# Six norms of a two-block transformer kernel, taken in two halves of the tokens

## The chip, the core and the metric

The kernel runs on one core of one Trainium2 chip. The metric is the time of one execution on the device in microseconds, and the median of the runs is what is compared. The engines are TensorE (PE, products), VectorE (DVE), ScalarE (ACT), GpSimd (POOL) and SyncE (SP, which issues the loads). They run side by side and wait for one another by semaphores only.

## What is computed

512 tokens of width 1024 pass through a block with a convolution mixer and a pooling mixer, and then through a block with a Fourier mixer, a feed-forward layer, a retention mixer with four heads, a second feed-forward layer and a final norm. The context branch of the reference doesn't reach the output and isn't computed. Cut to what matters here:

```python
def _rms(x, g):
    return x * lax.rsqrt(jnp.mean(x * x, axis=-1, keepdims=True) + EPS) * g

# between two mixers, six times (n1 to n6; n0 is the one at the start):
x = x + gate[:, None, :] * (y @ w_out)                 # leaves the last product of a stage
h = rmsnorm(x, norm_g) * (1.0 + scale[:, None, :]) + shift[:, None, :]
... = h @ w_in                                          # first product of the next stage

# gate, scale and shift come from a product of the condition vector:
mod = silu(c) @ w_ada[i] + b_ada[i]
```

## The kernel before

Everything lies transposed: x is [128, 8, 512], eight chunks of 128 features by 512 tokens. Every operand of a product is kept as two float32r parts, hi and lo, and a product is three matmuls, hi by hi, hi by lo, lo by hi (`three`, L1278 to L1280). An output tile is 128 features by 512 tokens in one PSUM bank, eight chunks of features deep, that is 24 matmuls of 512 columns. Four banks are in use at a time, so tiles come in fours (`four_tiles`). The last part of a feed-forward layer is six chunks deep, the last retention projection four, with two tiles in a unit.

Weights come in units of 128 x 1024, four slots. SyncE loads a unit into w_raw, ScalarE rounds it to w_hi (`refill`, L516), GpSimd subtracts to get w_lo (L425). `refill(name, s)` fills the slot that tile s of `name` has left, and stands in ScalarE's own order where the code writes it. The modulation vectors are summed by VectorE from groups of four 512 KB blocks (`sum_mods`, L892), each group loaded into the ring that the group before it leaves; these calls stand between VectorE's evictions.

A stage ends in `out`: TensorE makes eight tiles (the first four with their chunks interleaved, as the input comes), VectorE adds each to x (L921), ScalarE squares it (L525), VectorE adds the square to ssum (L856). Then `stat` brings the sums to one number per token (L1335), ScalarE takes the root, VectorE the reciprocal and four diagonals (L864), `spread` brings them back over the partitions into ps_bc (L1353), and `norm` makes for each chunk m_buf (L877, one input in PSUM), h_hi on ScalarE (L541) and h_lo (L881, both tensor inputs in SBUF). The next stage's first four tiles follow the chunks as they come (`h_part`). `keep_busy` issues products whose result nobody reads (L1329), one at a statistic and two behind a spread.

What follows a norm is the pooling stage (n1; VectorE's window sums, which ScalarE's refills wait for), the Fourier stage (n2; its products go through `ab_hi`, `ab_lo`, L1105), feed-forward (n3, n5), retention (n4; `rotary`, L1172 on) and the output (n6; L820 and eight stores). The order on each engine is the order in which the code is written; nothing reorders it.

## Time and profile before

| | us |
|---|---|
| median of 3 runs | 1791.09 |
| lowest, highest | 1789.49, 1798.33 |
| profiled execution | 1794.07 |
| its span | 1792.3 |
| PE busy in the span | 1682.2 |
| DVE busy | 896.0 |
| ACT busy | 588.0 |
| POOL busy | 753.9 |

A busy share is an average over stages that have different limits. What one stage could gain is read from the stretches in which the fullest engine waits, and from what ends those waits. The granted clock of TensorE over the span was 0.962 of full speed. A line number is that of the kernel before; the line of a helper serves many places.

### The profile page before, as it was taken

Reading aid. Unit: us, or ns where it says so; the run is one execution under the profiler, and the core shown is the slowest. Engines: PE = TensorE matmul, PEld = TensorE weight load, DVE = VectorE, ACT = ScalarE, POOL = GpSimd, SP = SyncE. Lnnn points to the kernel's source line nnn. Section 1 sums busy time; section 2 is a strip of 40 time slices with the busy share of each in tenths; the row PEclk is TensorE's granted clock in tenths of the full one; section 3 lists DMA queues with packets and bytes.
Section 4 is the critical chain, followed back from the end, with each engine's and each line's share of the span. In section 5 each row is a group of like instructions: output and inputs, shape, how many; then the busy total and the mean of one; then the engine's idle time right before and its main releaser. Section 6 shows DMA issues by size and latency. Waiting matters only on the chain.

```text
span 1792.3 us, 21415 instructions
## 1 busy us (share of the span) xinstructions
PE 1682.2 (94%) x7244; PEld 1355.9 (76%) x7244; DVE 896.0 (50%) x1369; ACT 588.0 (33%) x772; POOL 753.9 (42%) x354
## 2 busy tenths in 40 slices
PE   6999598899798999999998999999999899999997
PEld 4786386777666888888886878888787688888886
DVE  7999888876457534333357245171543511111114
ACT  4434442243222432222233333342333342222233
POOL 4799431454024344444444323334232253544442
PEclk8999698999898999999998999999999899999999
DMA  7431254376046455555552222222121132322321
GB/s 296 167 141 59 94 205 165 126 248 225 24 141 235 166 197 188 188 187 202 177 195 94 81 71 78 85 82 92 60 93 48 47 106 82 117 94 85 112 77 56
DMA packets 65149, 232.31 MB, mean 130 GB/s; under 512 B 7232, under 2 KB 7232, under 8 KB 64960
## 3 DMA queue, kind: packets, MB, share of 16 engines
q1 hardware_dynamic: 65088, 231.50, 37.6%
q8 instruction: 38, 0.62, 0.1%
q14 instruction: 23, 0.19, 0.0%
HBM read 229.38 MB, written 2.10 MB: 129 GB/s over the span
## 4 chain that ended last, share of the span: by engine, by line
issue 61%; POOL 26%; PE 2%; POOLq 1%; ACT 0%; DVE 0%; DVEq 0%
POOL w_lo L425 25%; POOL cv_y L498 1%; PE bank L1278 1%; PE bank L1279 1%; PE bank L1280 1%; POOLq L424 0%; POOLq L501 0%; ACT x L820 0%; POOL cv_y L491 0%; DVE m_buf L877 0%; PE ps_bc L1353 0%; PE ps_stat L1335 0%; PE ps_bc L1329 0%; DVE x L921 0%; ACT sq L525 0%
## 5 line engine op out<-in xcount | busy, mean ns | idle before, releaser
L425 POOL TENSOR_TENSOR w_lo<-w_raw,w_hi 128x1024 fp32r<-128x1024 f32 x272 | 662.2, 2440 | 995.0 <-ACT w_hi L516 974.7
L1278 PE MATMUL bank<-h_hi,w_hi 128*128 128x512 f32 x1344 | 531.4, 395 | 18.6 <-POOL w_lo L425 11.7
L1279 PE MATMUL bank<-h_lo,w_hi 128*128 128x512 f32 x1344 | 526.3, 392 | 0.0
L1280 PE MATMUL bank<-h_hi,w_lo 128*128 128x512 f32 x1344 | 526.2, 392 | 0.0
L516 ACT ACTIVATE w_hi<-w_raw 128x1024 fp32r<-128x1024 f32 x268 | 281.4, 1052 | 272.1 <-PE bank L1280 252.1
L1278 PEld LDWEIGHTS bank<-h_hi,w_hi 128*128 128x128 f32 x1344 | 254.4, 189 | 81.5 <-POOL w_lo L425 15.7
L1280 PEld LDWEIGHTS bank<-h_hi,w_lo 128*128 128x128 f32 x1344 | 254.2, 189 | 53.9
L1279 PEld LDWEIGHTS bank<-h_lo,w_hi 128*128 128x128 f32 x1344 | 254.4, 189 | 53.5 <-issue 1.1
L1278 PE MATMUL bank<-f_hi,w_hi 128*128 128x512 f32 x624 | 246.4, 395 | 8.7 <-POOL w_lo L425 4.0
L1279 PE MATMUL bank<-f_lo,w_hi 128*128 128x512 f32 x624 | 245.3, 393 | 0.0
L1280 PE MATMUL bank<-f_hi,w_lo 128*128 128x512 f32 x624 | 244.8, 392 | 0.0
L1144 DVE TENSOR_TENSOR z_buf<-bank,s_buf 128x512 f32<-128x512 f32 x44 | 30.4, 692 | 314.0 <-PE bank L1280 314.0
L892 DVE CUSTOM_DVE_ANT_0 mods_ring<-mods_ring,c_all 128x1024 f32<-128x1024 f32 x144 | 167.7, 1214 | 7.3 <-DMA mods_ring<-w_mods_in 7.0
L546 ACT ACTIVATE f_hi<-z_buf 128x512 fp32r<-128x512 f32 (+1 forms) x100 | 62.7, 630 | 283.8 <-DVE z_buf L1144 190.9
L921 DVE SCALAR_TENSOR_TENSOR x<-bank,mod,x 128x512 f32<-128x512 f32 x80 | 59.8, 747 | 174.3 <-PE bank L1280 174.3
L1278 PEld LDWEIGHTS bank<-f_hi,w_hi 128*128 128x128 f32 x624 | 118.4, 190 | 36.4 <-POOL w_lo L425 5.7
L1280 PEld LDWEIGHTS bank<-f_hi,w_lo 128*128 128x128 f32 x624 | 118.7, 190 | 25.1
L1279 PEld LDWEIGHTS bank<-f_lo,w_hi 128*128 128x128 f32 x624 | 118.7, 190 | 24.5
L913 DVE TENSOR_TENSOR f_lo<-z_buf,f_hi 128x512 fp32r<-128x512 f32 (+1 forms) x100 | 80.9, 810 | 52.1 <-ACT f_hi L546 50.8
L525 ACT ACTIVATE sq<-x 128x512 f32<-128x512 f32 x48 | 30.3, 632 | 153.5 <-DVE x L921 153.5
L1005 DVE SCALAR_TENSOR_TENSOR ps_bc<-cv_y,vec,ps_bc 128x512 f32<-128x512 f32 (+1 forms) x111 | 74.8, 674 | 0.0
L1005 DVE SCALAR_TENSOR_TENSOR ps_stat<-cv_y,vec,ps_stat 128x512 f32<-128x512 f32 (+1 forms) x111 | 74.8, 674 | 0.0
(177 smaller groups left out, 1520.1 us busy)
## 6 DMA issues: line engine op xcount, KB each, us to landing
mods_ring<-w_mods_in SPq DMA_DIRECT2D x152, 512.0 KB, 5.9
w_raw<-ff_in_in SPq DMA_DIRECT2D x88, 512.0 KB, 3.3
w_raw<-ret_in SPq DMA_DIRECT2D x64, 512.0 KB, 3.3
w_raw<-ff_out_in SPq DMA_DIRECT2D x32, 512.0 KB, 3.3
w_raw<-cv_ab_in SPq DMA_DIRECT2D x16, 512.0 KB, 5.2
w_raw<-ff_tail_in SPq DMA_DIRECT2D x16, 384.0 KB, 3.1
w_raw<-cv_g_in SPq DMA_DIRECT2D x8, 512.0 KB, 3.3
w_raw<-cv_out_in SPq DMA_DIRECT2D x8, 512.0 KB, 5.3
```

The source lines that it names most:

```text
L425: pool.tensor_tensor(w_lo[:, s, :], w_raw[:, s, :], w_hi[:, s, :].bitcast(F32), ALU.subtract).then_inc(lo_done, 1)
L516: act.activation(w_hi[:, u % SLOTS, :], w_raw[:, u % SLOTS, :], ACT.Copy).then_inc(hi_done, 1)
L525: act.activation(sq[:], src, ACT.Square).then_inc(sq_ready, 1)
L546: act.activation(dst, z_buf[:, q, :], ACT.Copy).then_inc(zh_ready, 1)
L892: v.tensor_tensor_reduce(out=mods_ring[:, s, :], in0=mods_ring[:, s, :], in1=c_all[:], scale=1.0, scalar=0.0, op0=ALU.mult, op1=ALU.add, a ...
L913: v.tensor_tensor(dst, z_buf[:, q, :], hi, ALU.subtract).then_inc(zl_ready, 1)
L921: v.scalar_tensor_tensor(x[:, j, :], bank[j % SLOTS][:], gate(n, j), x[:, j, :], ALU.mult, ALU.add).then_inc(left[j % SLOTS], 1)
L1005: v.scalar_tensor_tensor(acc(q, n), cv_y[:, bass.ds(k + (c * ROW + a), n)], vec[:, bass.ds(DC * k + (V_DW + c), 1)], acc(q, n), ALU.mult, ...
L1144: v.tensor_tensor(z_buf[:, q, :], bank[2 * q + 1][:], s_buf[:, q, :], ALU.mult).then_inc(left[2 * q + 1], 1)
L1278: pe.matmul(out, w_h, m_h, start=start, stop=False)
L1279: pe.matmul(out, w_h, m_l, start=False, stop=False)
L1280: return pe.matmul(out, w_l, m_h, start=False, stop=stop)
```

## The change

The tokens are handled in two halves of 256 at n1 to n6. The last four tiles of a stage's last product are made for tokens 0 to 255 first (two tile halves in one bank) and then for tokens 256 to 511. Behind the first half, VectorE and ScalarE evict, square and normalise the first half of the tokens, while TensorE makes the second half, with the statistic and the spread of the first half between its tile halves. The next stage's first four tiles are made for the first half of the tokens, in pairs of banks, with the statistic and the spread of the second half between them, and then for the second. The filler products at the six norms go. The modulation sums that stood ahead of every second or fourth tile stand ahead of the first two or four tiles, group 9 is loaded earlier, and the Fourier stage makes its tiles in another order (`ab_place`). The six are n1 to n6, by the map OUT_OF. The core of the diff:

```diff
+HALF = [slice(0, HT), slice(HT, T)]
+OUT_OF = {"cv_out": 1, "pl_out": 2, "fr_out": 3, "out02": 4, f"ro{HEADS - 1}": 5, "out12": 6}
@@ sync
             mods(8)
+            mods(9)
             four(later("pl_v", 0), t["pl_v"], 0)
...
-            mods(9)
...
-            for c in range(DC):
-                sp.wait_ge(out_ready, c + 1)
-                sp.dma_start(t["y_t"][:, c, :], x[:, c, :]).then_inc(y_out, 16)
+            for hf in range(2):
+                for c in range(0, DC, 2):
+                    sp.wait_ge(out_ready, DC * hf + c + 2)
+                    sp.dma_start(t["y_t"][:, c:c + 2, HALF[hf]], x[:, c:c + 2, HALF[hf]]).then_inc(y_out, 16)
@@ scalar
+            def out_and_norm(name, per_unit=1):
+                n = OUT_OF[name]
+                load_table(ACT.Sqrt)
+                for j in range(SLOTS):
+                    wait_left(act, name, j)
+                    square(f"n{n}", j, x[:, j, :])
+                    if j % per_unit == per_unit - 1:
+                        refill(name, j // per_unit)
+                half_squares(name, 0)
+                half_std(n, 0)
+                if per_unit == 1:
+                    refill(name, 4)
+                norm_part(n, 0, 0, 3)
+                refill(name, 5 if per_unit == 1 else 2)
+                norm_part(n, 0, 3, 6)
+                if per_unit == 1:
+                    refill(name, 6)
+                norm_part(n, 0, 6, 8)
+                refill(name, 7 if per_unit == 1 else 3)
+                half_squares(name, 1)
+                half_std(n, 1)
+                norm_part(n, 1, 0, DC)
@@ vector
+            def half_norm(n, hf):
...
+                for c in range(DC + 1):
+                    if c < DC:
...
+                        v.scalar_tensor_tensor(m_buf[:, c % 2, h], x[:, c, h], aff[:, c:c + 1], ps_bc[:, h],
                                                ALU.mult, ALU.mult).then_inc(m_ready, 1)
+                    if c and n < 6:
+                        v.wait_ge(hh_ready, H0[n] + DC * hf + c)
+                        v.scalar_tensor_tensor(h_lo[:, c - 1, h], m_buf[:, (c - 1) % 2, h],
                                                mod[:, SHIFT[n] + c - 1:SHIFT[n] + c],
+                                               h_hi[:, c - 1, h].bitcast(F32), ALU.add,
                                                ALU.subtract).then_inc(hl_ready, 1)
...
+            def out_and_norm(name, gate_of, per_unit=1, g=None):
+                n = OUT_OF[name]
+                for j in range(SLOTS):
+                    if g:
+                        sum_mods(g.pop(0))
+                    wait_unit(v, name, j // per_unit)
+                    v.scalar_tensor_tensor(x[:, j, :], bank[j][:], gate(gate_of, j), x[:, j, :],
+                                           ALU.mult, ALU.add).then_inc(left[j], 1)
+                    add_square(f"n{n}", j)
+                prepare(n)
+                for hf in range(2):
+                    h = HALF[hf]
+                    for p in range(2):
+                        b, j = 2 * hf + p, SLOTS + 2 * p
+                        if hf == 0:
+                            v.wait_ge(half_done, 2 * (n - 1) + p + 1)
+                        else:
+                            wait_unit(v, name, (j + 1) // per_unit)
+                        for e in range(2):
+                            v.scalar_tensor_tensor(x[:, j + e, h], bank[b][:, HALF[e]], gate(gate_of, j + e),
+                                                   x[:, j + e, h], ALU.mult,
+                                                   ALU.add).then_inc(left[b] if e else x_half, 1)
+                        half_square_sum(f"n{n}", hf, 2 * p)
+                        if p == 0:
+                            half_square_sum(f"n{n}", hf, 1)
+                    half_norm(n, hf)
...
-            out("cv_out", 0, "n1", g=6, every=2)
-            norm(1, ST["n1"])
+            out_and_norm("cv_out", 0, g=[6, 7, 8, 9])
...
-            out("pl_out", 1, "n2", g=16)
+            out_and_norm("pl_out", 1, g=[16, 17])
...
-            out("fr_out", 2, "n3", g=19, every=2)
+            out_and_norm("fr_out", 2, g=[19, 20, 21, 22])
...
+                        out_and_norm(f"out{layer}{p}", n, g=None if g is None else [g, g + 1])
@@ tensor
-                if name[0] == "n" and name != "n0":
-                    keep_busy(BUSY["std"], ps_bc)
+            def last_half_tiles(name, a_hi, a_lo, chunks=DC, per_unit=1):
+                n = OUT_OF[name]
+                for hf in range(2):
+                    h = HALF[hf]
+                    for e in range(4):
+                        b = 2 * hf + e // 2
+                        unit, off = (e, 0) if per_unit == 1 else (2 + e // 2, 4 * (e % 2))
+                        if hf == 0 and e % per_unit == 0:
+                            unit_ready(name, unit if per_unit == 2 else SLOTS + e)
+                        if e % 2 == 0:
+                            bank_ready(name, SLOTS + b)
+                        for k in range(chunks):
+                            w = slice((off + k) * P, (off + k + 1) * P)
+                            last = three(bank[b][:, HALF[e % 2]], w_hi[:, unit, w], w_lo[:, unit, w],
+                                         a_hi[:, k, h], a_lo[:, k, h], k == 0, k == chunks - 1)
...
+                        if hf and e == 0:
+                            half_stat(n, 0)
+                        if hf and e == 1:
+                            half_spread(n, 0)
+            def first_half_tiles(name, n):
...
+                for pair in ((0, 1), (2, 3)):
+                    for k in range(DC):
+                        pe.wait_ge(hl_ready, H0[n] + k + 1)
+                        tiles(k, pair, 0)
+                        if pair == (2, 3) and k == DC // 2 - 1:
+                            half_spread(n, 1)
+                    if pair == (0, 1):
+                        half_stat(n, 1)
+                for k in range(DC // 2):
+                    pe.wait_ge(hl_ready, H0[n] + DC + k + 1)
+                    tiles(k, range(SLOTS), 1)
+                for s in range(SLOTS):
+                    for k in range(DC // 2, DC):
+                        if s == 0:
+                            pe.wait_ge(hl_ready, H0[n] + DC + k + 1)
+                        last = tiles(k, (s,), 1)
+                    last.then_inc(unit_used, 1)
...
-            stat("n4")
-            spread(ST["n4"])
-            keep_busy(BUSY["norm"], ps_stat)
```

## Rows read from the trace of the kernel before

**Rows 1.** The page, parts 1 and 5: busy, mean ns, idle before.
```profile
PE 1682.2 (94%) x7244; PEld 1355.9 (76%) x7244; DVE 896.0 (50%) x1369; ACT 588.0 (33%) x772; POOL 753.9 (42%) x354
...
L425 POOL TENSOR_TENSOR w_lo<-w_raw,w_hi 128x1024 fp32r<-128x1024 f32 x272 | 662.2, 2440 | 995.0 <-ACT w_hi L516 974.7
...
L516 ACT ACTIVATE w_hi<-w_raw 128x1024 fp32r<-128x1024 f32 x268 | 281.4, 1052 | 272.1 <-PE bank L1280 252.1
...
L892 DVE CUSTOM_DVE_ANT_0 mods_ring<-mods_ring,c_all 128x1024 f32<-128x1024 f32 x144 | 167.7, 1214 | 7.3 <-DMA mods_ring<-w_mods_in 7.0
...
L525 ACT ACTIVATE sq<-x 128x512 f32<-128x512 f32 x48 | 30.3, 632 | 153.5 <-DVE x L921 153.5
```
**Rows 2.** Windows: length, busy by engine (instructions), PEclk, DMA share, GB/s.
```profile
269.40:286.10 16.70, 9.90 (x32) 6.67 (x31) 13.86 (x23) 4.79 (x7) 4.66 (x2) 0.69 0.55 199
450.70:461.40 10.70, 7.38 (x31) 4.81 (x29) 6.57 (x13) 3.62 (x6) 2.35 (x1) 0.73 0.31 98
565.00:583.30 18.30, 9.81 (x31) 6.71 (x31) 15.68 (x24) 4.80 (x7) 8.34 (x4) 0.63 0.68 233
943.20:954.00 10.80, 8.45 (x30) 5.19 (x30) 8.57 (x12) 4.19 (x7) 5.94 (x3) 0.68 0.50 174
1402.90:1418.10 15.20, 9.65 (x30) 6.92 (x30) 8.55 (x17) 5.42 (x8) 4.68 (x2) 0.66 0.33 104
1778.30:1792.30 14.00, 3.92 (x27) 2.89 (x25) 7.67 (x16) 6.41 (x10) 0.00 (x0) 0.80 0.41 150
```
**Rows 3.** Timeline of VectorE at n4 (start, us); groups by form (128x256).
```profile
920.79 0.75 DVE L921 SCALAR_TENSOR_TENSOR x<-bank,mod,x 128x512 f32<-128x512 f32 x1 [3.63 <-PE bank L1280]
...
951.70 1.41 DVE L877 SCALAR_TENSOR_TENSOR m_buf<-x,aff,ps_bc 128x512 f32<-128x512 f32 x2 [1.65 <-PE ps_bc L1353]
...
961.92 1.63 DVE L881 SCALAR_TENSOR_TENSOR h_lo<-m_buf,mod,h_hi 128x512 fp32r<-128x512 f32 x2
...
L1005 DVE SCALAR_TENSOR_TENSOR ps_bc<-cv_y,vec,ps_bc 128x256 f32<-128x256 f32 x29 | 14.0, 484 | 0.0
```
**Rows 4.** Windows, 512 columns; timeline of TensorE, 256 columns, 40 starts apart.
```profile
405.00:410.00 5.00, 5.00 (x23) 4.11 (x23) 4.63 (x6) 1.68 (x3) 2.46 (x1) 1.00 0.79 263
...
463.07 0.28 PE L1279 MATMUL bank<-fr_lo,h_hi 128*128 128x256 f32 x1
...
467.73 0.28 PE L1280 MATMUL bank<-fr_hi,h_lo 128*128 128x256 f32 x1
```
**Rows 5.** Timelines of VectorE and GpSimd, at n3, n5 and n4.
```profile
576.00 2.26 DVE L839 SCALAR_TENSOR_TENSOR aff<-mod,vec 128x8 f32<-128x8 f32 x1
...
573.57 4.66 POOL L425 TENSOR_TENSOR w_lo<-w_raw,w_hi 128x1024 fp32r<-128x1024 f32 x2 [4.89 <-ACT w_hi L516]
...
1409.17 0.17 DVE L839 SCALAR_TENSOR_TENSOR aff<-mod,vec 128x8 f32<-128x8 f32 x1
...
926.12 0.74 DVE L921 SCALAR_TENSOR_TENSOR x<-bank,mod,x 128x512 f32<-128x512 f32 x1
...
923.24 10.86 POOL L425 TENSOR_TENSOR w_lo<-w_raw,w_hi 128x1024 fp32r<-128x1024 f32 x4 [8.27 <-ACT w_hi L516]
```
**Rows 6.** Timelines of VectorE and TensorE behind n4, n1 and n2.
```profile
970.99 0.69 DVE L1172 TENSOR_TENSOR m_buf<-bank,rot 128x512 f32<-128x512 f32 x1 [7.36 <-PE bank L1280]
...
983.97 0.80 PE L1278 MATMUL bank<-w_hi,h_hi 128*128 128x512 f32 x1 [4.93 <-DVE m_buf L1178]
...
309.34 0.70 DVE L1067 TENSOR_TENSOR pl_s<-pl_v 128x527 f32<-128x527 f32 x1
...
316.49 0.80 PE L1278 MATMUL bank<-h_hi,w_hi 128*128 128x512 f32 x1 [2.89 <-POOL w_lo L425]
...
471.72 0.36 PE L1278 MATMUL bank<-fr_hi,h_hi 128*128 128x256 f32 x1 [3.71 <-DVE ab_lo L1105]
...
481.80 0.47 PE L1278 MATMUL bank<-w_hi,ab_hi 128*128 128x512 f32 x1 [2.35 <-DVE ab_lo L1105]
```
**Rows 7.** Timeline of ScalarE, the last instruction of the kernel's n6.
```profile
1788.44 1.38 ACT L820 ACTIVATE x<-m_buf,mod 128x512 f32<-128x512 f32 x2 [0.16 <-DVE m_buf L877]
```

More of the change, by code:

```diff
@@ L660, in _ @@
                     hi(f_hi[:, c - 1, :], (c - 1) % 2)
-            out("cv_out", "n1")
-            std(ST["n1"], D)
-            norm(1)
+            out_and_norm("cv_out")
             for j in range(DC):
@@ L711, in _, with ffn @@
             refill("fr_2", 3)
-            out("fr_out", "n3")
-            std(ST["n3"], D)
-            norm(3)
-            def ffn(layer, stat):
+            out_and_norm("fr_out")
+            def ffn(layer):
                 for p, n in enumerate(PARTS):
@@ L806, in _ @@
                 hi(f_hi[:, j, :], j % 2)
-            name = f"ro{HEADS - 1}"
-            load_table(ACT.Sqrt)
-            for j in range(DC):
-                wait_left(act, name, j)
-                square("n5", j, x[:, j, :])
-                if j % 2:
-                    refill(name, j // 2)
-            std(ST["n5"], D)
-            norm(5)
-            ffn(1, "n6")
-            std(ST["n6"], D)
-            for c in range(DC):
-                act.wait_ge(m_ready, DC * 6 + c + 1)
-                act.activation(x[:, c, :], m_buf[:, c % 2, :], ACT.Identity,
-                               bias=mod[:, SHIFT[6] + c:SHIFT[6] + c + 1]).then_inc(out_ready, 1)
+            out_and_norm(f"ro{HEADS - 1}", per_unit=2)
+            ffn(1)
         @block.vector
@@ L865, in spread @@
                                     ALU.mult).then_inc(diag_ready, 1)
-            def norm(n, stat, lo=True):
-                prepare(n)
-                spread(stat)
+            def half_norm(n, hf):
+                s = SD[f"n{n}"] + hf
+                h, two = HALF[hf], slice(2 * hf, 2 * hf + 2)
+                v.wait_ge(std_ready, s + 1)
+                v.reciprocal(rstd[:, two], stdev[:, two]).then_inc(rstd_ready, 1)
+                v.wait_ge(rstd_ready, s + 1)
+                for j in range(2 * hf, 2 * hf + 2):
+                    v.tensor_scalar(diag[:, j * P:(j + 1) * P], ident[:], rstd[:, j:j + 1], None,
+                                    ALU.mult).then_inc(diag_ready, 1)
@@ L1265, in _ @@
             head_center(h)
-            spread(h + ST["h0"])
+            spread(h + SD["h0"])
             head_result(h, 0, Z0[f"y{h}"])
-            out(f"ro{h}", 4, "n5", per_unit=2)
-            norm(5, ST["n5"])
-            ffn(1, 5, "n6")
-            norm(6, ST["n6"], lo=False)
+            out_and_norm(f"ro{h}", 4, per_unit=2)
+            ffn(1, 5)
         @block.tensor
@@ new lines, in first_half_tiles, with tiles @@
+            def first_half_tiles(name, n):
+                def tiles(k, units, hf):
+                    for s in units:
+                        if k == 0 and hf == 0:
+                            unit_ready(name, s)
+                            bank_ready(name, s)
+                        w = slice(k * P, (k + 1) * P)
+                        last = three(bank[s][:, HALF[hf]], w_hi[:, s, w], w_lo[:, s, w], h_hi[:, k, HALF[hf]],
+                                     h_lo[:, k, HALF[hf]], k == 0, k == DC - 1)
+                    return last
+                for pair in ((0, 1), (2, 3)):
[14 more added lines that the diff above has]
+                        last = tiles(k, (s,), 1)
+                    last.then_inc(unit_used, 1)
@@ L1367, in spread_c, with out @@
+            def out(name, a_hi, a_lo, ready, together=SLOTS, chunks=DC):
+                four_tiles(name, 0, a_hi, a_lo, chunks, ready=ready, together=together)
+                last_half_tiles(name, a_hi, a_lo, chunks)
             def spread_c(n):
@@ L1410, in _ @@
             out("cv_out", f_hi, f_lo, z_part("cv"))
-            stat("n1")
-            spread(ST["n1"])
-            keep_busy(BUSY["norm"], ps_stat)
             for name in ("pl_v", "pl_g"):
                 for b in range(2):
-                    four_tiles(name, SLOTS * b, h_hi, h_lo, ready=h_part(1) if (name, b) == ("pl_v", 0) else None)
+                    if (name, b) == ("pl_v", 0):
+                        first_half_tiles(name, 1)
+                    else:
+                        four_tiles(name, SLOTS * b, h_hi, h_lo)
                     if (name, b) == ("pl_v", 1):
@@ L1470, in _ @@
             out("fr_out", f_hi, f_lo, z_part("fr"), together=2)
-            stat("n3")
-            spread(ST["n3"])
-            keep_busy(BUSY["norm"], ps_stat)
             def ffn(layer, n):
@@ L1478, in ffn @@
                     if p == 0:
-                        four_tiles(name, 0, h_hi, h_lo, ready=h_part(n))
+                        first_half_tiles(name, n)
                     with pe.Fori(1 if p == 0 else 0, chunks // 2) as i:
                         four_tiles(name, 0, h_hi, h_lo, i=i)
+                    if p == len(PARTS) - 1:
+                        out(f"out{layer}{p}", f_hi, f_lo, z_part(f"f{layer}{p}"), together=2, chunks=chunks)
+                        continue
                     four_tiles(f"out{layer}{p}", 0, f_hi, f_lo, chunks, ready=z_part(f"f{layer}{p}"),
@@ L1575, in result @@
                     last.then_inc(tile_done, 1)
-            four_tiles("qk0", 0, h_hi, h_lo, ready=h_part(4))
+            first_half_tiles("qk0", 4)
             v_units(0, 0, range(4))
```

194 lines of the change are left out of this document (119 added, 75 removed).

## Prediction

> **What bounds the kernel now.** I read the engine table first: TensorE is busy for 94% of the span [rows 1], so a change pays only where TensorE waits. Next I cut the span at the six norms, with one stretch of the windows view each, from the last product ahead of a norm to the first one behind it (the last stretch runs to the end of the trace). They are 16.7, 10.7, 18.3, 10.8, 15.2 and 14.0 us, 85.7 us in all [rows 2]. I call them n1 to n6. The reader should see two things there. What TensorE does in them is short, at a granted clock of 0.63 to 0.80, so they are nearly all loss; and VectorE is the busy engine. This is the pool from which the change can take.
>
> The chain in a stretch is: add to x, square, sum, statistic, reciprocal, diagonal, spread, multiply, h_hi, h_lo. One pass of eight chunks takes 11.8 us on VectorE, 1.45 us a chunk, from the first m_buf to the last h_lo [rows 3].
>
> **Splitting the products** costs next to nothing. At full clock 512 columns take 5.00/22 = 0.227 us from start to start, and 256 columns take (467.73-463.07)/40 = 0.1165 us [rows 4], 6 ns more for the pair. Some 860 products of 512 columns are split, so 5 us over the kernel; the times below are made with 0.1165.
>
> **Removed and added on TensorE.** The filler products (3 per norm, in two passes each) go. They lie inside the 85.7 us. Two half statistics (1.0 us each) and two half spreads (0.6 us each) replace one of each.
>
> **What moves, worked out at n4** (six chunks a tile). Before, the products of out02 end at 943.2, so the first four tiles end 72 x 0.227 = 16.4 us earlier, at 926.8. The first x leaves at 920.8 [rows 3]. Now the second group of modulation sums stands ahead of tile 1 and not of tile 4: 4 x 1.14 = 4.7 us (1.21 each, overlapping by 0.08) [rows 1]. So tile 1 leaves at 927.4. Its unit is refilled only behind that: square 0.63, w_hi 1.05, w_lo 2.4 [rows 1], at 932.2. The next two w_lo follow on GpSimd at 3.0 us each with what is between them. Tile halves e1, e2, e3 of the first half start at 932.2, 935.2 and 938.2, and the first half ends at 940.4. TensorE would have been there at 935.2: 5 us of weights that nothing hides.
>
> The second half then takes 8.4 us, with statistic and spread 10.0 us: the products end at 950.4, 7 us later than now. VectorE starts the first half norm when the spread is done, at 946.1. A 256-column scalar_tensor_tensor takes 0.48 us [rows 3], 0.40 behind another, so a chunk of two of them and its wait for ScalarE takes 0.93 and eight chunks 8 us from the spread.
>
> **The step that decides** is what GpSimd does meanwhile. On ScalarE the refills of the next four units now stand at the start, after three and six chunks and at the end of the first half norm, so their w_lo (2.4 us each) run beside the h_lo, which before had GpSimd to themselves. At n3 GpSimd ran two w_lo from 573.57 for 4.66 us; an aff of 8 columns, with two SBUF inputs, took 2.26 us and ended with the second. With GpSimd idle the same instruction took 0.17 us [rows 5]. The eviction of x, whose one input is PSUM, kept 0.74 us beside four w_lo [rows 5]. h_lo reads m_buf and h_hi, both in SBUF, so I cost each w_lo that meets an h_lo at up to its whole length; a bound below is nothing, since no h_lo lies beside a w_lo in this trace. I take the upper value, because aff is the same instruction with the same kind of operands. The Trainium skill (GPSIMD Engine Reference, section 1, Specifications) says the same against this change: GpSimd shares its SBUF interfaces with VectorE, with contention where a VectorE instruction has two SBUF inputs. By that rule, the trace agrees (2.26 against 0.17 us).
>
> So chunks 3, 6 and 7 wait 2.0, 2.1 and 2.3 us and the pass ends at 960.3, not 954.1. Behind it on VectorE are queued the four second-half evictions and their sums (3.1 us); TensorE stands at the second half statistic from 961, until 963.5. The statistic ends at 964.5, four chunks of the second pair run, spread at 967.9, second half norm to 975.7. TensorE finishes the first four tiles of the next stage at 982.0; before it was 954.0+21.9+0.3 = 976.2. That is +5.8.
>
> And these four tiles end 1.4 us apart instead of 2.7, because their last half has half columns. The next stage's VectorE work starts when tile 1 is done: 979.2 against 970.99, and TensorE already waited for it (4.93 us, until 983.97) [rows 6]. So **n4: +8.2**, and 0.3 for a stretch at half clock after these waits, 8.5.
>
> **The others, by the same steps.**
> n1: four groups of sums (6 to 9) now stand ahead of tiles 0 to 3, each 4.7 us and bound by the load that its predecessor frees. Tile 3 leaves at 262.2, its weights come at 266.5, the first half ends at 269.3, where before all products had ended. Spread 276.3, first half norm to 290.6, second to 306.0. Before, the norm ended 9.5 us behind the first product (as 963.5 to 954.0 at n4), at 295.6. The windows of the pool stage start 13.7 us behind that, at 309.34, and TensorE already waits for them (weights whose refill is queued behind them, 2.89 us) [rows 6]. So **+10**.
> n2: first half norm to 462.5, spread at 468.3, second half norm to 476.2; only then does VectorE evict the Fourier products, for whose banks the second half waits. It starts at 477.1 instead of 471.72 and then needs about the 10.1 us that it needs now [rows 6]: 5.4, less 1 as its last wait of 2.35 us has two banks and not four before it. **+4.5**.
> n3: first half at 563.1, norms to 584.4 and 599.8, first four tiles at 606.0 against 605.2. Tile 0 is now free 4.2 us before the end of the four, not 8.2, and table load, silu, w_hi and w_lo need 5.3: 1.1 us. With 0.6 for the clock **+2.5**.
> n5: no sums, four chunks. VectorE is last as before: statistic 1405.9, norms to 1417.9 and 1435.2, four tiles at 1441.5 against 1440.3, then the same 1.1 and 0.7: **+3**.
> n6: no next stage. Products end at 1782.0 instead of 1778.3, first half norm at 1782.4, evictions 3 us, second statistic 1786.0, last x 1792.4 against 1789.8 [rows 7]: **+2.5**.
>
> **Sum:** 10 + 4.5 + 2.5 + 8.5 + 3 + 2.5 = 31 us. The profiled execution took 1794.07 us around a span of 1792.3; the median is 1791.09, 3 us less. 1791.1 + 31 = 1822. I take the other reordering (loads of group 9 ahead of pl_v, output in eight half pieces of the same size) at nothing: the load queue is ahead of its users there, and each piece still moves 256 KB; if not, 2 us.
>
> **Rivals.**
> A. *No collision.* h_lo of two SBUF inputs runs beside w_lo, or the w_lo fall into gaps. Then the same steps give first half norms of 8 us, and n1 +4, n2 -2.5, n3 -4, n4 +1, n5 -4.5, n6 +1: -5, **1786**. For it: h_lo was never seen beside w_lo. Against: aff [rows 5]. It is not slower than before; it decides from the point where a w_lo costs an h_lo under 0.3 us.
> B. *Part of it.* Sums and diagonals wait, h_lo hardly: n1 +6.5, n2 +1, n3 -2, n4 +4.5, n5 +0.5, n6 +2.5: +13, **1804**.
> C. *The waits vanish*: half a norm hides behind half the products, weights come in time. Of 85.7 us the two half statistics and spreads and the splitting leave 4.5 each, at n6 all but 4; with half of the weights' waits some 45 us are gained: **1746**. For it: VectorE is free between evictions. Against it: the refills hang on tiles 1 to 3 behind the sums, and n6 is one serial chain.
> That a stage is not halved at all I exclude; all six calls are in the diff.
>
> **Chances.** Forecast (1808 to 1842) 0.58, A 0.15, B 0.15, C 0.10, longer still 0.02. The range leaves out C and the ends of A and of the longer case: 1775 to 1842. A measurement of this kernel tells about 0.5%, 9 us, from no change. Faster by more: C and a third of A, 0.16. Within: the rest of A and part of B, 0.16. Slower: 0.68.
>
> **What would show it.** In the trace after: h_lo of 128x256 at 0.48 us with some at over 2 us ending with a w_lo; a first half norm of 14 us from its spread and a second of 8; TensorE idle for 2 us and more ahead of the second to fourth half tiles at n1, n3 and n4, released by w_lo; the second half of the Fourier products released by ab_lo; the first pool window after 318. Wrong would be: first half norms of 8 us (A), products of n4 ended before 945 (C), or pool windows at 310.

## The result and the profile after

The changed kernel took 1839.33 us (median of 4 runs, 1838.08 to 1842.22), before 1790.29 (4 runs): 1.0279 times the time, 95% interval 1.0256 to 1.0301, so 2.6 to 3.0% slower. The profiled execution has a span of 1836.3 us (before 1792.3) at a mean granted clock of 0.956 (before 0.962).

The page of the changed kernel, parts 1 and 5 (busy, mean ns, idle before), answers to [rows 1]:

```profile
PE 1683.6 (92%) x8076; PEld 1404.8 (77%) x8076; DVE 934.4 (51%) x1505; ACT 605.5 (33%) x850; POOL 753.2 (41%) x354
...
L438 POOL TENSOR_TENSOR w_lo<-w_raw,w_hi 128x1024 fp32r<-128x1024 f32 x272 | 661.5, 2438 | 1036.0 <-ACT w_hi L529 1016.0
...
L529 ACT ACTIVATE w_hi<-w_raw 128x1024 fp32r<-128x1024 f32 x268 | 281.3, 1051 | 259.8 <-PE bank L1358 246.6
...
L929 DVE SCALAR_TENSOR_TENSOR h_lo<-m_buf,mod,h_hi 128x256 fp32r<-128x256 f32 x80 | 63.0, 791 | 3.9 <-ACT h_hi L556 3.0
```

TensorE is busy for as long as before (1683.6 against 1682.2 us) in a span 44 us longer. The 32 filler matmuls of the six norms (0.59 to 1.20 us each) went, and the second passes and stretches at a lower clock took their place; on top of that TensorE waits more. The work of GpSimd and ScalarE on weights is the same to 1 us. The one line that stands out is h_lo: 791 ns on average for 256 columns, where an instruction of the same kind and size that reads PSUM takes 484 [rows 3].

TensorE's waits in the changed kernel (line waited at, releaser: us in all, times, longest):

```profile
PE bank L1356 <- POOL w_lo L438: 40.3, 22, 9.1
PE ps_stat L1446 <- DVE ssum L939: 18.8, 6, 5.5
...
PE bank L1356 <- DVE m_buf L1258: 11.7, 5, 7.2
PE bank L1356 <- DVE ab_lo L1184: 10.5, 2, 8.6
PE bank L1356 <- DVE h_lo L929: 8.5, 7, 1.5
PE bank L1356 <- DVE x L961: 6.7, 2, 6.0
```

Timelines (start, us) of VectorE, GpSimd and TensorE at n4 in the changed kernel:

```profile
943.04 0.75 DVE L948 SCALAR_TENSOR_TENSOR x<-bank,mod,x 128x512 f32<-128x512 f32 x1 [3.63 <-PE bank L1358]
972.03 2.36 POOL L438 TENSOR_TENSOR w_lo<-w_raw,w_hi 128x1024 fp32r<-128x1024 f32 x1 [2.72 <-ACT w_hi L529]
972.39 2.28 DVE L929 SCALAR_TENSOR_TENSOR h_lo<-m_buf,mod,h_hi 128x256 fp32r<-128x256 f32 x1
976.76 4.89 POOL L438 TENSOR_TENSOR w_lo<-w_raw,w_hi 128x1024 fp32r<-128x1024 f32 x2 [2.37 <-ACT w_hi L529]
977.12 4.83 DVE L929 SCALAR_TENSOR_TENSOR h_lo<-m_buf,mod,h_hi 128x256 fp32r<-128x256 f32 x2
...
979.49 0.39 PE L1356 MATMUL bank<-h_hi,w_hi 128*128 128x256 f32 x1 [0.84 <-DVE h_lo L929]
982.00 0.56 PE L1356 MATMUL bank<-h_hi,w_hi 128*128 128x256 f32 x1 [1.52 <-DVE h_lo L929]
985.23 0.98 PE L1446 MATMUL ps_stat<-ones,ssum 128*128 128x1 f32 x4 [1.60 <-DVE ssum L939]
986.07 0.99 PE L1450 MATMUL ps_stat<-ones,sq 128*128 128x1 f32 x4
992.19 0.66 PE L1458 MATMUL ps_bc<-diag,ones 128*128 128x128 f32 x4
...
1018.15 0.79 PE L1356 MATMUL bank<-w_hi,h_hi 128*128 128x512 f32 x1 [7.17 <-DVE m_buf L1258]
```

An h_lo that meets a w_lo ends some 0.3 us behind it: 972.39 + 2.28 = 974.67 beside 972.03 + 2.36 = 974.39, and the pair at 977.12 runs to 981.95, the two w_lo to 981.65. Over the whole trace 13 of the 80 h_lo started beside a running w_lo and took 2.28 to 2.58 us; the others took 0.48.

TensorE has a second loss, which no wait shows. Between the statistic's end (987.06) and the spread (992.19) lie 24 products of 256 columns, 24 x 0.1165 = 2.8 us at full clock; they took 5.1. Windows of the changed kernel (length, busy, PEclk, DMA share, GB/s) around it, and of the same 24 products at n1, n3 and n5:

```profile
978.65:986.92 8.27, 4.30 (x21) 3.83 (x21) 6.14 (x9) 1.62 (x4) 3.01 (x2) 0.71 0.41 127
986.92:992.39 5.47, 5.47 (x27) 5.47 (x28) 0.65 (x3) 0.26 (x1) 0.00 (x0) 0.51 0.00 0
992.39:1007.00 14.61, 14.61 (x124) 14.61 (x123) 9.67 (x20) 7.15 (x11) 2.84 (x2) 1.00 0.01 2
...
295.20:299.91 4.71, 4.71 (x25) 4.71 (x25) 0.65 (x3) 0.26 (x1) 0.00 (x0) 0.56 0.57 231
606.60:611.10 4.50, 4.50 (x26) 4.50 (x27) 0.65 (x3) 0.26 (x1) 0.00 (x0) 0.62 0.00 0
...
1459.91:1464.29 4.38, 4.38 (x26) 4.38 (x26) 0.65 (x3) 0.26 (x1) 0.00 (x0) 0.61 0.00 0
```

A granted clock of 0.51 is the lower of the two levels (1.2 GHz) nearly throughout.

Where the 44 us arose is read from one event that both kernels have, the first eviction of x (512 columns) in each matrix: cv_out, pl_out, fr_out, out00, out02, the first head's, the last head's, out10, out12, and the last instruction of ScalarE. A stage runs from one event to the next, and each of n1 to n6 lies in the stage that has its name. The heads' stage (first head's event to the last head's) holds none of the six; neither do the two that are left out, out00 to out02 and out10 to out12, which took 236.5 us each before and after. In us, with the experiments below (e11: n5 and the heads together 411.6, as e10's 411.4):

```
                      n1     n2     n3    n4    heads   n5     n6    all
before              179.6  114.2  149.1  186.7  283.2  128.8  33.9
changed             191.6  120.2  154.0  199.1  281.7  136.0  37.5
e1 fillers          189.6  121.4  153.2  195.7  283.3  133.8  37.0  1830.6
e2 m in PSUM        191.4  120.1  153.9  195.4  281.8  134.8  36.5  1834.7
e3 copies first     184.1  121.7  152.2  200.0  281.7  136.0  35.7  1828.7
e4 tile by tile     192.0  119.7  157.3  198.5  281.9  137.3  37.5  1842.5
e5 all whole        180.8  111.2  148.9  187.0  283.3  128.1  35.3  1792.8
e6 only n6 halved   179.7  111.3  149.0  186.9  283.2  128.1  37.5  1794.3
e7 e1+e2+e3         182.5  121.2  149.2  192.6  281.8  131.8  35.3  1813.0
e8 last sums late   177.6  113.6  145.6  187.0  283.2  128.1  35.4  1785.5
e9 e7, n2 whole     189.2  112.5  149.2  192.5  281.8  131.8  35.4  1810.1
e10 e8 + loads      176.1  112.9  141.7  186.9  283.3  128.1  35.4  1778.6
e11 e10 + fillers   172.7  112.2  141.5  186.9    411.6       34.1  1775.1
```

The last column is the median of the runs; the runs of before beside them had medians of 1792.4 (e1 to e4), 1791.0 (e5 to e8) and 1790.1 (e9 to e11). One execution of before beside e5 to e8 took 5879.5 us and is not in the ratios. The first event differs by up to a few us from run to run, so a sum of stages and a span can differ by that.

### The profile page after: what moved, and what is told of

Its sections match the earlier page's. It is cut to its first block, busy times and chain, and to the rows that moved or that the text cites. A ratio compares the mean times of both kernels' runs of the same rounds, so it can differ in the third digit from the quotient of the medians.

```text
span 1836.3 us, 23334 instructions
## 1 busy us (share of the span) xinstructions
PE 1683.6 (92%) x8076; PEld 1404.8 (77%) x8076; DVE 934.4 (51%) x1505; ACT 605.5 (33%) x850; POOL 753.2 (41%) x354
## 4 chain that ended last, share of the span: by engine, by line
issue 63%; POOL 25%; PE 1%; POOLq 1%; DVE 0%; ACT 0%; ACTq 0%; DVEq 0%
POOL w_lo L438 25%; POOL cv_y L511 1%; POOLq L437 0%; POOLq L514 0%; ACT x L559 0%; DVE m_buf L925 0%; POOL cv_y L504 0%; PE bank L1356 0%; PE bank L1357 0%; PE bank L1358 0%; PE ps_bc L1458 0%; PE ps_stat L1450 0%; PE ps_stat L1446 0%; DVE ssum L939 0%; ACT sq L575 0%
## 5 line engine op out<-in xcount | busy, mean ns | idle before, releaser
L1356 PE MATMUL bank<-h_hi,w_hi 128*128 128x512 f32 (+1 forms) x1504 | 565.4, 376 | 37.5 <-POOL w_lo L438 20.2
L1357 PE MATMUL bank<-h_lo,w_hi 128*128 128x512 f32 (+1 forms) x1504 | 558.7, 371 | 0.0
L1358 PE MATMUL bank<-h_hi,w_lo 128*128 128x512 f32 (+1 forms) x1504 | 558.1, 371 | 0.0
L1357 PEld LDWEIGHTS bank<-h_lo,w_hi 128*128 128x128 f32 x1504 | 289.8, 193 | 47.0 <-issue 1.0
L1358 PEld LDWEIGHTS bank<-h_hi,w_lo 128*128 128x128 f32 x1504 | 289.5, 192 | 47.4
L1356 PE MATMUL bank<-f_hi,w_hi 128*128 128x512 f32 (+1 forms) x752 | 272.2, 362 | 25.4 <-POOL w_lo L438 20.2
L1357 PE MATMUL bank<-f_lo,w_hi 128*128 128x512 f32 (+1 forms) x752 | 269.3, 358 | 0.0
L1358 PE MATMUL bank<-f_hi,w_lo 128*128 128x512 f32 (+1 forms) x752 | 269.1, 358 | 0.0
L1004 DVE SCALAR_TENSOR_TENSOR x<-bank,mod,x 128x512 f32<-128x512 f32 x32 | 24.0, 751 | 124.2 <-PE bank L1358 124.2
L929 DVE SCALAR_TENSOR_TENSOR h_lo<-m_buf,mod,h_hi 128x256 fp32r<-128x256 f32 x80 | 63.0, 791 | 3.9 <-ACT h_hi L556 3.0
```

The lines of the kernel that those rows point to most:

```text
L929: v.scalar_tensor_tensor(h_lo[:, c - 1, h], m_buf[:, (c - 1) % 2, h], mod[:, SHIFT[n] + c - 1:SHIFT[n] + c], h_hi[:, c - 1, h].bitcast(F32 ...
L1004: v.scalar_tensor_tensor(x[:, j, :], bank[j % SLOTS][:], gate(n, j), x[:, j, :], ALU.mult, ALU.add).then_inc(left[j % SLOTS], 1)
L1356: pe.matmul(out, w_h, m_h, start=start, stop=False)
L1357: pe.matmul(out, w_h, m_l, start=False, stop=False)
L1358: return pe.matmul(out, w_l, m_h, start=False, stop=stop)
```

## Experiments

**e1, fillers.** Does the half clock cost, or is it only seen?

```
 for k in range(DC):
+    if pair == (0, 1) and k >= 6: half_busy(n, k - 5)
     pe.wait_ge(hl_ready, H0[n] + k + 1)
 ...
 if pair == (0, 1):
+    half_busy(n, 4)
     half_stat(n, 1)
+half_busy(n, m):  m x matmul(ps_stat[:, HALF[1]], ones, vec[:, 0:HT])
```

> The changed kernel (1839.3 us, span 1836.3) with fillers for TensorE: at the four norms whose next stage starts with half tiles (n1, n3, n4, n5) TensorE multiplies ones into an unused part of the statistic's bank, 1 matmul of 256 columns after the sixth chunk, 2 after the seventh, 4 ahead of its wait for the second half's statistic. Theory A (the half clock after these waits is the term that my sum sized too small): the four statistic matmuls take 0.50 us instead of 0.99 and the 24 products ahead of the second spread 2.8 to 3.1 us instead of 5.0, 4.6, 5.5 and 4.7, so 2 to 3 us come back at each of the four norms: 1828 to 1832 us, and the granted clock rises from 0.956. Rival B (the next wait takes the gain: rotation, pool windows or w_lo are what ends there): the 24 products are as short as in A but the time stays at 1837 to 1841. Rival C (the fillers are longer than the waits): 1840 to 1845.

1830.58 us, 1.0205 times before (1.0191 to 1.0219); the changed kernel is at 1.0279. Timeline and windows of TensorE at n4 in this run:

```profile
981.94 1.89 PE L1491 MATMUL ps_stat<-vec,ones 128*128 128x256 f32 x8
984.35 0.58 PE L1446 MATMUL ps_stat<-ones,ssum 128*128 128x1 f32 x4 [0.52 <-DVE ssum L939]
988.20 0.61 PE L1458 MATMUL ps_bc<-diag,ones 128*128 128x128 f32 x4
```

```profile
977.63:985.24 7.61, 6.04 (x37) 4.65 (x35) 6.29 (x9) 1.62 (x4) 3.15 (x2) 1.00 0.46 138
985.37:988.20 2.83, 2.83 (x25) 2.83 (x25) 0.65 (x3) 0.26 (x1) 0.00 (x0) 1.00 0.00 0
```

Granted clock 1.00 throughout, and the 24 products take 2.8 us at all four norms. The stages of n4, n5, n1 and n3 came down by 3.4, 2.2, 2.0 and 0.8 us. Theory A holds for the mechanism. For its size the readings differ: the two profiled spans differ by 5.4 us (n2 and the heads took some back, and the profiled run of e1 is the slowest of its five), the medians as they stand by 8.7, and the ratios to before by 13 us with some 5 either way.

**e2, m in PSUM.** Is it the operands that make h_lo wait for w_lo?

```
+m_of = lambda n: c_all (two banks, as [P, 2, T]) if n >= 4 else m_buf
-v.scalar_tensor_tensor(m_buf[:, c % 2, h], x[:, c, h], aff[:, c:c + 1], ps_bc[:, h], ...)
+v.scalar_tensor_tensor(m_of(n)[:, c % 2, h], x[:, c, h], aff[:, c:c + 1], ps_bc[:, h], ...)
```

and m_of(n) likewise where h_hi, h_lo and the output read m.

> The changed kernel with the scaled chunk m of the norms n4, n5 and n6 in the two PSUM banks that the modulation sums have left, so that h_lo of n4 and n5 reads one operand of SBUF (h_hi) and one of PSUM. Theory A (an instruction of VectorE with two SBUF inputs stands still as long as a GpSimd instruction runs): h_lo of n4 and n5 takes 0.5 us everywhere, none of 2.28 and 4.83/2; the first half's norm ends 4 us sooner at n4 and 2 us at n5, the waits of TensorE for h_lo (0.84, 1.52 us) and a part of that for the statistic go: 3 to 5 us at n4, 1 to 3 at n5, 1831 to 1836 us in all. h_lo of n1 and n3, still in SBUF, keeps its 2.3 us instances. Rival B (it is a shared queue or clock and not the operands): h_lo of n4 keeps its 2.3 us instances, 1838 to 1841. Rival C (a PSUM operand makes every m and h_lo longer): more than 0.6 us each, 1840 to 1845.

1834.68 us, 1.0236 (1.0222 to 1.0250). Groups of VectorE by form (count | busy, mean ns | idle before), and the timelines at n4:

```profile
L931 DVE SCALAR_TENSOR_TENSOR h_lo<-m_buf,mod,h_hi 128x256 fp32r<-128x256 f32 x48 | 40.1, 841 | 2.3 <-ACT h_hi L558 1.7
L931 DVE SCALAR_TENSOR_TENSOR h_lo<-c_all,mod,h_hi 128x256 fp32r<-128x256 f32 x32 | 15.4, 480 | 1.2 <-ACT h_hi L558 1.1
```

```profile
971.62 2.38 POOL L440 TENSOR_TENSOR w_lo<-w_raw,w_hi 128x1024 fp32r<-128x1024 f32 x1 [2.67 <-ACT w_hi L531]
971.94 0.48 DVE L931 SCALAR_TENSOR_TENSOR h_lo<-c_all,mod,h_hi 128x256 fp32r<-128x256 f32 x1
```

The same instruction in the same program: 480 ns in all 32 places with one operand in PSUM, eight of them beside a running w_lo (as 971.94 within 971.62 to 974.00); 841 ns on average with both in SBUF. Theory A holds, n4 -3.7 and n5 -1.2 us. TensorE's waits for h_lo at n4 are gone. A part was lost again: the sum of squares, which still has both operands in SBUF, met a w_lo instead, 2.44 us at 977.29 (n4) and 2.26 at 1448.09 (n5), where it takes 0.43. The Trainium skill (GPSIMD Engine Reference, section 1, Specifications) names VectorE instructions with two SBUF inputs among those that contend with GpSimd; this run agrees, 480 against 841 ns.

**e3, copies first.** Who delays the first half's weights?

```
 for j in range(SLOTS):
+    if j % per_unit == per_unit - 1: refill(name, j // per_unit)
     wait_left(act, name, j)
     square(f"n{n}", j, x[:, j, :])
-    if j % per_unit == per_unit - 1: refill(name, j // per_unit)
```

> The changed kernel, and in ScalarE's order at the first four tiles of each last matrix the copy w_hi of the next weights stands ahead of the wait for the tile's eviction and its square, not behind them. Theory A (the first half's waits for weights, 7.7 us at n1, 5.7 at n3, 3.2 at n4, come from the modulation sums: VectorE's four sums delay the eviction, this the square, this the copy, this w_lo): these waits go, and at n1 and n3 TensorE then waits for the first half's statistic, which still stands behind the sums (266.9 us in the profile of the changed kernel, 5.1 us before TensorE's own time for it), so n1 gains about 5 us, n3 about 4 and n4 2 to 3: 1826 to 1830 us. Rival B (GpSimd or the transfer of the raw weights is late anyway): TensorE's waits for w_lo at the half tiles stay at 7.7 and 5.7 us, 1837 to 1841. Rival C (the squares come later by the copy and with them everything behind): 1840 to 1845.

1828.68 us, 1.0211 (1.0192 to 1.0230). Timeline of TensorE at n1, of the changed kernel (three lines) and of this one:

```profile
252.49 0.38 PE L1356 MATMUL bank<-f_hi,w_hi 128*128 128x256 f32 x1 [2.69 <-POOL w_lo L438]
259.30 0.58 PE L1356 MATMUL bank<-f_hi,w_hi 128*128 128x256 f32 x1 [3.67 <-POOL w_lo L438]
266.15 0.39 PE L1356 MATMUL bank<-f_hi,w_hi 128*128 128x256 f32 x1 [1.37 <-POOL w_lo L438]
```

```profile
250.72 0.39 PE L1356 MATMUL bank<-f_hi,w_hi 128*128 128x256 f32 x1 [1.08 <-POOL w_lo L438]
257.50 0.58 PE L1356 MATMUL bank<-f_hi,w_hi 128*128 128x256 f32 x1 [3.64 <-POOL w_lo L438]
265.22 0.60 PE L1446 MATMUL ps_stat<-ones,ssum 128*128 128x1 f32 x4 [0.41 <-DVE ssum L939]
```

The total is A's. The stages are not: n1 came down by 7.5 us and n3 by 1.8, where A had about 5 and 4; n4 did not come down (199.1 to 200.0), where A had 2 to 3. The waits fell from 7.7 to 4.7 us at n1 and not to nothing: copy j+1 still stands behind the square of tile j, which waits for the modulation sums, so the order moved each copy up by one tile and no further. That the chain runs from the sums through eviction, square and copy to w_lo is shown; that the copy is all that is wrong with it is not.

**e4, tile by tile.** Does the next stage wait because the first four tiles end close together?

```
-for k in range(DC // 2):
-    pe.wait_ge(hl_ready, H0[n] + DC + k + 1)
-    tiles(k, range(SLOTS), 1)
 for s in range(SLOTS):
-    for k in range(DC // 2, DC):
+    for k in range(DC):
```

> The changed kernel, and the second half of the next stage's first four tiles is multiplied tile by tile, all eight chunks of one before the next, where it was chunks 0 to 3 of all four and then the rest. The tiles end 2.8 us apart instead of 1.4, the first 4.2 us and the second 2.8 us sooner, the last at the same time. Theory A (what follows waits for the first tiles' results: the pool windows 13.05 us late, the rotation at 1004.5 with TensorE waiting 7.17 us behind it, the weights' copies bunched): the rotation starts 2.8 us sooner, TensorE's wait of 7.17 falls to 4.4 to 5, the windows start 3 to 4 us sooner: 5 to 10 us in all, 1829 to 1834 us. Rival B (VectorE comes to these steps only when it has finished the second half's norm, or TensorE then waits for the second half's h_lo): 1837 to 1842 us.

1842.48 us, 1.0275 (1.0261 to 1.0289), no gain. Timelines of this run behind n4:

```profile
999.59 0.38 PE L1356 MATMUL bank<-h_hi,w_hi 128*128 128x256 f32 x1 [0.29 <-DVE h_lo L929]
1000.50 0.39 PE L1356 MATMUL bank<-h_hi,w_hi 128*128 128x256 f32 x1 [0.29 <-DVE h_lo L929]
1004.78 0.69 DVE L1252 TENSOR_TENSOR m_buf<-bank,rot 128x512 f32<-128x512 f32 x1 [3.59 <-PE bank L1358]
...
1017.90 0.79 PE L1356 MATMUL bank<-w_hi,h_hi 128*128 128x512 f32 x1 [4.72 <-DVE m_buf L1258]
```

Rival B, just above its range; n3 even took 3.3 us more in this profile. The rotation needs the first two tiles (`wait_unit` for tile 2 * half + 1). It starts at 1004.8, and at 1004.5 in the changed kernel: the order only changes what holds it up. In the changed kernel TensorE makes products without a gap from the second spread to 1007.0 (14.61 us busy of 14.61 in the window above) and ends the second tile on the way. Here the first tile goes at the pace of h_lo, with four waits of 0.29 us, until the last h_lo is done at 1001.1, and the 24 products of the second tile are still to come. TensorE's wait of 7.17 us became 4.7, but its tiles ended later.

**e5, all norms whole**, to see what the rest of the change does.

```
-HALVED = [f"n{n}" for n in range(1, 7)]
+HALVED = []
```

with before's code for a norm that is not in the list.

> All six norms whole again, with the fillers of the kernel before, but the change's other edits kept: the load of the modulation block 9 ahead of the weights of pl_v, and the table fr_hi and fr_lo split ahead of pl_out and not behind it. Theory A (the halves are the loss): the time of the kernel before, less up to 2 us, for VectorE waited 1.93 us for block 9 in front of tile 6 at the first norm: 1787 to 1793 us where before has 1790 to 1792. Rival B (the moved load or the moved split cost part of the 49 us): 1795 to 1805 us.

1792.84 us, 1.0016 (1.0004 to 1.0028). The halves are the loss. The two edits kept cost nothing that counts, but not for want of effects. n2 is 3.0 us shorter, and the table's split ahead of pl_out is the only edit there; 1.2 us of it lie ahead of the norm's first m_buf and are in e6, e8 and e10 too, but the rest is mostly gone in e8 (113.6), so that it comes from the split is not shown. n1 is 1.2 us longer, and there the statistic waits 10.28 us (6.75 in before), with the weights of pl_v now behind block 9 on the load queue. n6 is 1.4 us longer with the code of before: TensorE's granted clock between its statistic and the first m_buf was 0.62 (1777.10 to 1781.54), in before 1.00 (1780.10 to 1783.04).

**e6, only n6 halved.**

```
+HALVED = ["n6"]
```

> Only the last norm, n6, in halves, the other five whole. Nothing stands behind it, so no weights, no rotation and no queue can take part. In the profile of the changed kernel the stretch from the first eviction of out12 to the end was 37.5 us, against 33.9. Theory A (the costs of the six norms add up, each in its own stage): 3 to 4 us above the run with all norms whole, the stretch 37 to 38 us. Rival B (n6 loses only because of what the halved norms ahead of it leave behind): the stretch 33 to 35 us, no loss against the run with all norms whole.

1794.28 us, 1.0023 (1.0008 to 1.0039). The stage took 37.5 us, as in the changed kernel, against 35.3 in e5 and 33.9 in before: 2.2 to 3.6 us, with nothing halved ahead of it. By medians the loss against e5 is 1.4 us, too small to be told from none. So A's stage is right and its total unproven.

**e7, the three mends together.**

> The changed kernel with three mends at once: the fillers of e1, m in PSUM of e2, the copies first of e3. By the stages of the three profiles: n1 from 191.6 us to 182 to 184, n2 120 to 122, n3 from 154.0 to 151.5, n4 from 199.1 to 192, n5 from 136.0 to 132.5, n6 from 37.5 to 35.7. Theory A (the three causes are separate and add up): 1816 to 1820 us, still 1.4 to 1.7 per cent above before, since what is left is the products' second pass and the two statistics. Rival B (they remove the same time): 1824 to 1828 us. Rival C (halves pay once the three are mended): below 1792 us.

1813.04 us, 1.0127 (1.0111 to 1.0143). Theory A, and 3 us better than its range: more than half of the 2.8% is these three causes. Halves still lose 1.3%. The largest rest is n2 (+7.0 against before, +10.0 against e5). Timeline of TensorE there:

```profile
466.19 0.55 PE L1358 MATMUL bank<-fr_hi,h_hi 128*128 128x256 f32 x1 [5.97 <-DVE x L963]
...
483.90 0.55 PE L1358 MATMUL bank<-fr_hi,h_hi 128*128 128x256 f32 x1 [8.62 <-DVE ab_lo L1186]
```

A bank whose eviction is queued behind the first half's norm on VectorE, then four banks queued behind the second's.

**e9, e7 with n2 whole.**

```
+HALVED = ["n1", "n3", "n4", "n5", "n6"]
```

> The three mends of e7, and the second norm, n2, whole; n1, n3, n4, n5 and n6 in halves. In the profile of e7 TensorE waits 5.97 us at n2 for a bank, whose eviction VectorE has queued behind the first half's norm, and then 8.62 us for ab_lo, queued behind the second's; the stage took 121.2 us, against 111.2 in e5_whole. Theory A (n2 is the costliest of the halved norms once the three are mended): the stage returns to 111 to 113 us, and the whole to 1803 to 1807 us, 0.7 to 0.9 per cent above before. Rival B (what n1 left late is only met one stage later): the stage stays above 117 us, 1808 to 1813.

1810.12 us, 1.0105 (1.0090 to 1.0120). The stage of n2 fell by 8.7 us, to 112.5, as A says, but the one ahead of it grew by 6.7. So the total is in B's range without B's reason, for B had the stage of n2 above 117. The profiled run is the slowest of the five (1813.74 us), which may be part of that growth. In the pool stage the copy of pl_grp's weights waited for its load until 396.02 us (391.70 in e7, where the stage had begun 1.6 us sooner). Why the load came later is open.

**e8, whole norms, last sums late.** The profiles of before and e5 showed a loss that has nothing to do with halving.

```
-if g and j % every == 0: sum_mods(g[j // every])
+if g and j % every == 0 and not (len(g) == 4 and j == 6): sum_mods(g[j // every])
 ...
+if g and len(g) == 4: sum_mods(g[3])
 prepare(n)
```

> All norms whole as in e5_whole, and at n1 and n3 the fourth group of modulation sums, which stood in front of tile 6's eviction, comes behind tile 7's. The profile of before has TensorE waiting 6.75 us at n1 and 8.32 at n3 for the sum that tile 6 feeds, though its products were done (269.4 and 565.0 us at the latest, statistic at 276.2 and 573.3). Theory A (these two waits are the modulation sums', not the norm's): the statistic starts 5 us sooner at n1 and 7 at n3; the four sums (4.8 us) and the preparation then stand beside the statistic and reach 1 to 3 us past it, so 3 to 5 us come back at each: 1779 to 1786 us, below before. Rival B (the sums only move onto the path between the statistic and the first m): 1787 to 1793 us.

1785.53 us, 0.9973 (0.9961 to 0.9986). Timeline of TensorE at n1 in before (its products ended at 269.42):

```profile
276.17 1.87 PE L1335 MATMUL ps_stat<-ones,ssum 128*128 128x1 f32 x8 [6.75 <-DVE ssum L856]
```

and of ScalarE (n1, n3) and TensorE (n1) in e8:

```profile
267.88 1.06 ACT L536 ACTIVATE w_hi<-w_raw 128x1024 fp32r<-128x1024 f32 x1 [5.67 <-DMA w_raw<-pl_v_in]
558.97 1.06 ACT L536 ACTIVATE w_hi<-w_raw 128x1024 fp32r<-128x1024 f32 x1 [5.54 <-DMA w_raw<-ff_in_in]
...
274.72 1.87 PE L1469 MATMUL ps_stat<-ones,ssum 128*128 128x1 f32 x8 [6.05 <-DVE ssum L918]
```

At the upper end of A's range. n1 and n3 came down by 3.2 and 3.3 us against e5, n2 took 2.4 back. The statistic started 4.2 us sooner at n1 and 4.0 at n3, where A had 5 and 7, and still waited 6.05 us at n1: now the copy w_hi of the next weights waits for its load, and the square stands behind the copy.

**e10, the two loads moved as well.**

```
-mods(9)
 four(later("pl_v", 0), t["pl_v"], 0)
+mods(9)
 ...
-mods(22)
+four("in00", t["ff_in0"], 0)
+mods(22)
+mods(23)      # and the loop behind starts at 1
```

> e8 (all norms whole, the fourth sums behind tile 7 at n1 and n3) and two loads moved on the queue: modulation block 9 back behind the first weights of pl_v, block 22 behind the first weights of in00. In the profile of e8 the square of tile 4 and with it the statistic stood behind w_hi of the next stage, and that waited 5.67 us at n1 and 5.54 us at n3 for the raw weights, which the queue held behind a modulation block. Theory A: both waits go, the statistic starts 4 to 6 us sooner at n1 and 3 to 4 at n3; the sums and the preparation then end after it and give 2 to 3 us of that back: 1777 to 1782 us. Rival B (the bytes are the limit, not the order): the waits for w_raw stay over 4 us, 1784 to 1788 us.

1778.56 us, 0.9932 (0.9918 to 0.9946). Timeline of TensorE at n1 and n3:

```profile
265.91 1.05 PE L1473 MATMUL ps_stat<-ones,ssum 128*128 128x1 f32 x8 [0.42 <-DVE ssum L922]
...
556.24 0.95 PE L1473 MATMUL ps_stat<-ones,ssum 128*128 128x1 f32 x8
```

Theory A: both waits of w_hi for its load are gone with the same bytes in another order, so the order on the queue was the limit. n1 is 3.5 and n3 7.4 us below before. This version beats both kernels.

**e11, short fillers in the whole norms too.**

```
+short_busy({4: 3, 5: 8}.get(n, 0))
 pe.wait_ge(sum_step, SS0[f"n{n}"] + DC - 1)
 columns(ssum, True, False)
+short_busy(2)
 ...
 keep_busy(BUSY["std"], ps_bc)
+short_busy(1)
```

> e10 and short fillers of 256 columns for TensorE in every whole norm: 2 between the two parts of the statistic, 1 behind the filler that is there, and 3 at n4 and 8 at n5 ahead of the statistic (waits of 1.55 and 5.58 us in e5_whole). In e5_whole and e8 the columns' matmuls, fillers and spread of the norms stand at half clock (8 columns 1.87 us instead of 0.95, filler 2.06 instead of 1.10, spread 2.08 instead of 1.16). Theory A (the half clock costs before's norms too): 1.5 to 3 us less at n2, n4 and n5 each, less at n1 and n3 where the sums end last: 1770 to 1776 us. Rival B (VectorE ends last in each norm, with the square, the sums or the spread's multiplicands): the records are shorter and the time the same as e10 within 3 us.

1775.05 us, 0.9913 (0.9893 to 0.9932), the fastest, though its interval overlaps e10's. In the stages n2, n4 and n5 gave 0.7 us or less, which is B and not A. n6 fell by 1.3 us: from its statistic to the first m_buf the granted clock is 1.00 (1759.70 to 1763.04), in e10 0.61 (1763.70 to 1768.10). n1 fell by 3.4 us, which neither theory has; I did not find why.

## Why the prediction was right, step by step

Forecast 1822 (1775 to 1842), measured 1839.33: inside, on the slower side as the likeliest case said, but within 3 us of the upper end, so the width of the range had a part in it. Rivals A, B and C fall: h_lo meets w_lo (2.28 and 4.83 us), the first half norm of n4 takes 13.6 us from the spread (968.3 to 981.95), where A has 8, and with all three causes mended the kernel is still 1.3% slower than before.

The terms, forecast and measured against before by the stages: n1 +10, +12.0 (with cv_out's first tile as start; +11.4 from the start of the trace); n2 +4.5, +6.0; n3 +2.5, +4.9; n4 +8.5, +12.4, of which 1.5 came back in the heads; n5 +3, +7.2; n6 +2.5, +3.6. Every term has the right sign and every one is too small: 31 against 44. None made up for another.

**Up to the second statistic the steps held.** At n4 the tile behind the sums, the weights' waits (3.15 us once, where I had 5 in all), the h_lo that end with a w_lo, the evictions queued behind them: forecast end of the second statistic 964.5 + 22.2 (the shift by then) = 986.7, measured 987.06. The first half norms at n1 to n4 end within 0.7 us of the forecast, moved by where the stage began. That VectorE's instruction waits out a whole w_lo was read off one 8-column aff [rows 5], which was thin. The trace of before had more: of the 44 sums of squares of 512 columns (both operands in SBUF) just the 21 that started beside a running w_lo took 1.23 to 2.45 us, the others 0.69, as here beside the w_lo from 1394.91 to 1397.31:

```profile
1395.97 1.89 DVE L856 TENSOR_TENSOR ssum<-ssum,sq 128x512 f32<-128x512 f32 x1 [0.70 <-ACT sq L525]
```

e2 shows that it is the operands.

**The mis-sized term is the half clock.** I gave "0.3 for a stretch at half clock" at n4, 0.6 or 0.7 at n3 and n5, and nothing at n1. Behind waits of 0.84, 1.52 and 1.60 us TensorE ran the statistic and 24 products at the lower level: 0.8 (1.83 for 1.02 in e1) + 2.3 us (5.1 for 2.8) at n4, and the same 0.8 and 1.5 to 1.9 on the products at n1, n3 and n5. The change had taken out the fillers, and I had counted them only as work saved. e1 put fillers back, the clock (1.00) followed, and so did the distance from the last h_lo of the first half norm to that of the second. At n1, n3 and n4 my steps have 15.4 us for it; the changed kernel took 18.2, 17.8 and 18.7, e1 15.5 at each. At n5 they have 17.3; it took 19.7, e1 17.4.

**At n5** TensorE waited 5.54 us for the first half's sums, as it had for the whole sums before (5.57), and my steps had that. They did not have the half clock behind it: the first statistic took 0.9 us more than at full clock, the 12 products behind it 1.2 more (2.57 for 12 x 0.1165), the second statistic 0.8 and its 24 products 1.6. These 4.5 us are the 4.2 missed, within what such a sum can tell.

**At n2** one wait was missing: TensorE stood 5.97 us for a bank whose eviction was queued behind the first half's norm, and the second norm ended 3.2 us later than my steps have it. e7, with the other causes mended, has the same wait.

**At n1** the weights' waits were 7.7 us, each from the sums, as forecast; e3 took 7.5 us off the stage. What I had as the last link, the pool windows, came at 322.39 instead of 309.34, +13 where my steps have +10.4, and TensorE waited 9.1 us behind them (before 2.89 [rows 6]).

**At n4** I had named the close ends of the tiles as one reason for the late rotation, 8.2 us with the later products. It started 11.2 us later than before, counted from the stage's first event, and 8.1 later in e1: the rest is the half clock. With the tiles apart (e4) it started only 0.2 us sooner, so that part of the reason gives nothing to win by itself.

**The other reordering at nothing, "if not, 2 us"**: e5, 1.0016, right in sum, which is partly luck: n2 was 3 us shorter and n1 1 longer, and I had seen neither. The output in eight half pieces is not in e5 (it stores as before does) and was not tested by itself.

## What to carry to other kernels

Splitting a norm to hide it costs a second pass through every queue that the norm shares: before splitting, list what is queued behind each half on each engine, and price the waits at the clock that TensorE has after them. Look first at what the exposed norm really waits for: here 7 to 8 us of two of the six were modulation sums and a load ahead of the weights on the queue, and moving these (e10) took 0.7% off, where halving added 2.8%. Where VectorE must work beside GpSimd, an instruction like h_lo should have one of its two tensor operands in PSUM, and so should its neighbours, or the collision moves on to them (e2).
